# A hybrid attention encoder step: outputs split a head later, reordered steps, and the causal mask added by a product

## The reference, cut to what matters

```
ckv, krope = rmsnorm(lat[:256]), rope(lat[256:])      # lat = rmsnorm(x) @ kv_w_down
k = [ckv @ w_uk | krope] ; v = ckv @ w_uv              # 8 heads, 128 + 64 and 128
q = [q_nope | rope(q_rope)]                            # rmsnorm(q_lat) @ w_uq
s = q @ k.T * scale
s = where(k // 64 <= q // 64, s, -inf)                 # CHUNK = 64
o = softmax(s) @ v * silu(gate)
x = x + rmsnorm(o @ w_out)
```

## Time and profile before

| | |
|---|---|
| median of 3 runs | 616.34 us (614.62 to 617.09) |
| the profiled execution | 617.37 us |
| its span, first to last instruction | 615.6 us |
| busy: PE / PE weight loads | 594.4 (97%) / 571.0 (93%) |
| busy: DVE / ACT / POOL | 368.6 (60%) / 306.3 (50%) / 109.1 (18%) |
| chain that ended last | PE 83%, DVE 9%, ACT 4% |
| mean granted TensorE clock | 0.991 |

### The profile page before, as it was taken

The page is one execution under the profiler, slowest core; times in us unless marked ns, Lnnn a source line. Parts: engine busy times, 40 slices in busy tenths (PEclk is TensorE's granted clock), DMA queues, the critical chain, the costliest instruction groups (busy, mean ns, idle before and its releaser), DMA issues.

```text
span 615.6 us, 11638 instructions
## 1 busy us (share of the span) xinstructions
PE 594.4 (97%) x4446; PEld 571.0 (93%) x4446; DVE 368.6 (60%) x578; ACT 306.3 (50%) x616; POOL 109.1 (18%) x173
## 2 busy tenths in 40 slices
PE   7999999999999999999999999999999959999996
PEld 7999999999999999999999999989988858999996
DVE  5466567554554883257726567468888856754415
ACT  6877473462353472257425515346656627853311
POOL 0100010010020052236706400210000114400002
PEclk8999999999999999999999999999999979999999
DMA  8932362262252163333415322631110144857004
GB/s 290 349 100 69 120 205 70 78 205 69 78 182 92 55 248 123 87 114 126 137 52 154 106 69 69 176 103 30 35 53 18 52 170 138 286 177 274 1 2 172
DMA packets 64888, 75.96 MB, mean 123 GB/s; under 512 B 5568, under 2 KB 55872, under 8 KB 64704
## 3 DMA queue, kind: packets, MB, share of 16 engines
q1 hardware_dynamic: 64832, 75.20, 38.7%
HBM read 62.31 MB, written 10.78 MB: 119 GB/s over the span
## 4 chain that ended last, share of the span: by engine, by line
PE 83%; DVE 9%; ACT 4%; issue 2%; DMA 1%; POOL 0%; SPq 0%; DVEq 0%; ACTq 0%; POOLq 0%
PE bank L1661 25%; PE bank L1662 24%; PE bank L1663 24%; PE bank L1940 3%; ACT prob L1277 2%; DVE pT_lo L1335 1%; PE bank L1708 1%; DVE slab_lo L1335 1%; DVE qN_lo L1335 1%; DVE oT_lo L1335 1%; DVE kN_lo L1335 1%; DVE rows L1331 1%; ACT qS L1064 1%; PE bank L1931 1%; DMA stage<-in_v0g_dram 1%
## 5 line engine op out<-in xcount | busy, mean ns | idle before, releaser
L1661 PE MATMUL bank<-slab_hi,hat_hi 128*128 128x256 f32 (+2 forms) x560 | 161.3, 288 | 2.4 <-DVE slab_lo L1335 2.2
L1662 PE MATMUL bank<-slab_lo,hat_hi 128*128 128x256 f32 (+2 forms) x560 | 160.2, 286 | 0.0
L1663 PE MATMUL bank<-slab_hi,hat_lo 128*128 128x256 f32 (+2 forms) x560 | 160.1, 286 | 0.0
L1661 PEld LDWEIGHTS bank<-slab_hi,hat_hi 128*128 128x128 f32 x560 | 105.9, 189 | 3.9 <-DVE slab_lo L1335 2.6
L1663 PEld LDWEIGHTS bank<-slab_hi,hat_lo 128*128 128x128 f32 x560 | 106.3, 190 | 0.7
L1662 PEld LDWEIGHTS bank<-slab_lo,hat_hi 128*128 128x128 f32 x560 | 105.9, 189 | 0.7
L1335 DVE TENSOR_TENSOR slab_lo<-stage,slab_hi 128x1024 fp32r<-128x1024 f32 (+3 forms) x70 | 83.0, 1186 | 24.9 <-ACT slab_hi L1064 23.4
L1661 PE MATMUL bank<-hat_hi,slab_hi 128*128 128x320 f32 x256 | 79.2, 309 | 0.4 <-DVE krL L1335 0.4
L1662 PE MATMUL bank<-hat_lo,slab_hi 128*128 128x320 f32 x256 | 78.8, 308 | 0.0
L1663 PE MATMUL bank<-hat_hi,slab_lo 128*128 128x320 f32 x256 | 78.7, 308 | 0.0
L1064 ACT ACTIVATE slab_hi<-stage 128x1024 fp32r<-128x1024 f32 (+3 forms) x70 | 71.0, 1014 | 7.2 <-PE bank L1663 2.1
(11 more groups left out here) (326 smaller groups left out, 1326.1 us busy)
## 6 DMA issues: line engine op xcount, KB each, us to landing
stage<-in_a_w_in_dram SPq DMA_DIRECT2D x22, 512.0 KB, 5.0
st_s<-in_state_gla_dram SPq DMA_DIRECT2D x4, 1024.0 KB, 7.0
out_dram<-st_s SPq DMA_DIRECT2D x4, 1024.0 KB, 5.1
stage<-in_a_w_out_dram SPq DMA_DIRECT2D x8, 512.0 KB, 4.3
stage<-in_b_w_in_dram SPq DMA_DIRECT2D x8, 512.0 KB, 4.4
stage<-in_ckvT_dram SPq DMA_DIRECT2D x8, 512.0 KB, 4.1
stage<-in_cache_ckv_dram SPq DMA_DIRECT2D x8, 512.0 KB, 6.1
stage<-in_b_w_out_dram SPq DMA_DIRECT2D x8, 512.0 KB, 4.0
```

The source lines that it names most:

```text
L1661: pe.matmul(out, a[0], b[0], start=first, stop=False)
L1662: pe.matmul(out, a[0], b[1], start=False, stop=False)
L1663: return pe.matmul(out, a[1], b[0], start=False, stop=last)
```

## The change

1. The masked corner is no longer filled by DVE. After the five products of a query tile PE adds a sixth, of two constants of 128 x 128 in which only row 0 is not zero: ones for the first 64 queries, -2^120 for the last 64 keys. They lengthen the table `const_r` by 256 columns.
2. `Oh` h stands a head later, and `O` h behind the slab's low half.
3. `ct`, `cl` of streams 0 and 1 stand a head later. The last `qabs` stands ahead of the last `S`.
4. `st` 0 stands ahead of the last `O`; its scratch `spT` no longer shares memory with `pT`.
5. `glT` stands ahead of `g0` 2. `qT` 0 and `qT` 1 stand among the `cT`. `qn` 0 and `kh` 0 stand ahead of `vh` 1, 1 instead of behind it.

```
-CONST_R, NCONST_R = columns((("cum_p", P + 2), ("cum_s", P + 2)))
+CONST_R, NCONST_R = columns((("cum_p", P + 2), ("cum_s", P + 2), ("early", P), ("late", P)))
...
-    out += [("vg", 1), ("vg", 2), ("g0", 0), ("g0", 1), ("g0", 2), ("glT",), ...
+    out += [("vg", 1), ("vg", 2), ("g0", 0), ("g0", 1), ("glT",), ("g0", 2), ...
...
-    out += [("gb", 3, 0), ("cT", 0), ("cT", 1), ("gb", 3, 1), ("cT", 2), ("cT", 3)]
+    out += [("gb", 3, 0), ("cT", 0), ("cT", 1), ("qT", 0), ("gb", 3, 1), ("cT", 2), ("cT", 3), ("qT", 1)]
     load("uqr")
-    out += [("gb", 2, 0), ("cT", 4)] + [("qT", t) for t in range(NT)] + [("ldt",), ("gb", 2, 1)]
+    out += [("gb", 2, 0), ("cT", 4)] + [("qT", t) for t in range(2, NT)] + [("ldt",), ("gb", 2, 1)]
...
-    out += [("vh", 0, t) for t in range(NP)] + [("vh", 1, 0), ("vh", 1, 1)]
+    out += [("vh", 0, t) for t in range(NP)] + [("vh", 1, 0), ("qn", 0), ("kh", 0), ("vh", 1, 1)]
...
-        elif 4 <= h < 6:
-            out += [("ct", h - 4)]
+        elif 5 <= h < 7:
+            out += [("ct", h - 5)]
+        if h + 1 == HB - 1:
+            out += [("qabs", h + 1)]
...
-        if 0 <= h < HB - 1:
-            out += [("O", h), ("Oh", h)]
+        if 0 < h < HB:
+            out += [("Oh", h - 1)]
         if 0 <= h < 4:
             out += [("plo", ("hd", h + 4), 0)]
-        elif 4 <= h < 6:
-            out += [("cl", h - 4)]
+        elif 5 <= h < 7:
+            out += [("cl", h - 5)]
+        if 0 <= h < HB - 1:
+            out += [("O", h)]
...
+        out += [("st", b)] + [("zr", b + 2)] * (b + 2 < SB)
         if b == 0:
             out += [("O", HB - 1)]
-        out += [("st", b)] + [("zr", b + 2)] * (b + 2 < SB)
...
-                    link(dve.memset(row[0:P // 2, i0 * P:i0 * P + 2 * apart].rearrange("p (j n) -> p j n", n=apart)[:, :, P // 2:P], NEG))
...
-                        last = pe.matmul(o, qS[:, h, q], krL[:, keys], start=False, stop=True)
+                        pe.matmul(o, qS[:, h, q], krL[:, keys], start=False, stop=False)
+
+                        last = pe.matmul(bank[:, j, q], cst_r("early"), cst_r("late"), start=False, stop=True)
```

More of the change, by code:

```diff
@@ L135, in steps @@
     out += [("rq",), ("rr",), ("const",), ("piece", ("qk", 0), 0), ("gf",), ("gfh",), ("gfl",), ("plo", ("qk", 0), 0), ("vg", 0), ("gw",)]
-    out += [("vg", 1), ("vg", 2), ("g0", 0), ("g0", 1), ("g0", 2), ("glT",), ("g0x", 0), ("g0x", 1), ("piece", ("qk", 0), 1)]
+    out += [("vg", 1), ("vg", 2), ("g0", 0), ("g0", 1), ("glT",), ("g0", 2), ("g0x", 0), ("g0x", 1), ("piece", ("qk", 0), 1)]
     out += [("z", u) for u in Z_ORDER] + [("g0x", 2), ("qp", 0), ("plo", ("qk", 0), 1)]
@@ L225, in latent_layer @@
     load(("hd", 1))
-    out += [("vh", 0, t) for t in range(NP)] + [("vh", 1, 0), ("vh", 1, 1)]
+    out += [("vh", 0, t) for t in range(NP)] + [("vh", 1, 0), ("qn", 0), ("kh", 0), ("vh", 1, 1)]
     load(("hd", 2))
-    out += [("qn", 0), ("kh", 0), ("vh", 1, 2)]
+    out += [("vh", 1, 2)]
     prompt_heads(out, load)
@@ L239, in prompt_heads @@
             out += [("piece", ("hd", h + 4), 0)]
-        elif 4 <= h < 6:
-            out += [("ct", h - 4)]
+        elif 5 <= h < 7:
+            out += [("ct", h - 5)]
+        if h + 1 == HB - 1:
+            out += [("qabs", h + 1)]
         if h + 1 < HB:
-            out += [("S", h + 1, 0), ("S", h + 1, 1), ("N", h + 1, 0), ("N", h + 1, 1), ("qabs", h + 1)]
+            out += [("S", h + 1, 0), ("S", h + 1, 1), ("N", h + 1, 0), ("N", h + 1, 1)]
+        if h + 1 < HB - 1:
+            out += [("qabs", h + 1)]
         if h + 2 < HB:
@@ L252, in prompt_heads @@
             out += [("cr", 2), ("ss", 0)]
-        if 0 <= h < HB - 1:
-            out += [("O", h), ("Oh", h)]
+        if 0 < h < HB:
+            out += [("Oh", h - 1)]
         if 0 <= h < 4:
             out += [("plo", ("hd", h + 4), 0)]
-        elif 4 <= h < 6:
-            out += [("cl", h - 4)]
-        elif h == 6:
+        elif 5 <= h < 7:
+            out += [("cl", h - 5)]
+        if 0 <= h < HB - 1:
+            out += [("O", h)]
+        if h == 6:
             out += [("ot", 2)]
@@ L541, in program @@
         const_r = sb("const_r", [P, NCONST_R], fp32r)
-        place[0] += 8 * P
         gain = {n: sb("gain_" + n, [P, k]) for n, k in
@@ L655, in program @@
         prob = [sb(f"prob{i}", [P, NT, P]) for i in range(2)]
-        place[0] = temp_at
-        spT = sb("spT", [P, TOK])
         place[0] = prob_at
         sprob = [sb("sprob1", [P, NT, P])]
+        spT = sb("spT", [P, TOK])
         place[0] = prob_at + 2 * 4 * NT * P
@@ L1614, in _ @@
                     _, h, u = step
-                    i0, i1 = UNITS[u]
-                    apart = 512 + (i1 - i0) * P
-                    link(dve.memset(row[0:P // 2, i0 * P:i0 * P + 2 * apart].rearrange("p (j n) -> p j n", n=apart)[:, :, P // 2:P], NEG))
                     for j, i in enumerate(UNITS[u]):
@@ L1980, in constants @@
     const = [np.eye(P), before, before * same, (i[:, None] // SL % 2 == np.arange(2)[None, :]), np.cos(ang), np.sin(ang)]
-    const_r = [cum_p, cum_s]
+    row = (i == 0).astype(np.float32)[:, None]
+    const_r = [cum_p, cum_s, row * (1 - half.T * 0 - (i >= P // 2)[None, :]), row * np.where(i >= P // 2, NEG, 0.0)[None, :]]
     return [np.ascontiguousarray(np.concatenate(x, axis=1).astype(np.float32)) for x in (const, const_r, turned[:1], turned[1:])]
```

## The result

The changed kernel takes 619.91 us (median of 7 runs, 617.58 to 621.91), the kernel before in the same session 615.47 (7 runs, 614.48 to 617.09). The ratio is 1.0058, 95% interval 1.0034 to 1.0082: slower, by 0.6%. The forecast was 614.8 with a range of 611.6 to 618.8. The profiled execution of the changed kernel has a span of 618.2 us, the one before 615.6.

The account below looks back on a forecast made before the run. PE was taken as the bound, busy 594 of 615.6 us. Heads -1.1, tail -3.5, projections +4.1, prologue -0.5 and `qn` 0, `kh` 0 -0.5 sum to -1.5: 614.8 us from the median 616.34, range 611.6 to 618.8.

Parts of the forecast that it names:

- What bounds the kernel: Whole kernel: PE busy 594 of 615.6 us; almost all its long waits lie where the change works.
- The mask as a product: PE gains 32 products, 0.45 us a head, 3.6 in all (bounds 1.8 and 8.6); DVE loses 16 memsets.
- rival C: Mask products cost PE 0.27 us each instead of 0.11, 5 us more: 619.8; chance 0.06.
- The heads: Heads 0 to 5: PE becomes the bound at 11.33 us, gain 1.6, less 0.45 for `S` 0's masks: -1.1.
- rival D: DVE's list still bounds the heads, which stay at 11.7 us, no gain of 1.6: 616.4; chance 0.10.
- `T` 6 to `sv` 0: Tail: 27.1 us becomes 23.6, old waits replaced by 6.5 us of new ones: -3.5, bounds -5.5 and -1.5.
- rival A: Clock falls at the projections' new wait, +2.4 to +3.4, up to 618.2; tail waits likewise, +2.4 each; chance 0.20.
- The MLA projections: `gb` 3, 1 takes the banks of `gb` 3, 0, so PE idles 3.3 us: +4.1, bounds +5 and 0.
- The prologue: Start: `g0` 2 covers `glT`'s read-out, a wait of 0.90; `glT` itself waits some 0.35: -0.5.
- `qn` 0 and `kh` 0: Ahead of `S` 0: a step earlier, the wait of 0.46 for `kN_lo` goes, covered by a `vh`: -0.5.
- The sum: Whole kernel: -1.1 - 3.5 + 4.1 - 0.5 - 0.5 = -1.5, giving 614.8 from the median; chance 0.50.

Follow-up runs that it names:

- e10: The kernel before with only `Oh` h a head later and `O` h behind the slab's low half; 610.32 us, ratio 0.9913 to the kernel before.
- e7: e3 with the mask by DVE's memset again and the sixth product left out; 607.98 us, ratio 0.9867 to the kernel before.
- e6: The kernel before with the mask product in place of the memset and nothing else; 614.95 us, ratio 0.9986 to the kernel before.
- e3: The changed kernel with `glT` and `qT` 0, 1 both back in their old places; 611.73 us, ratio 0.9919 to the kernel before.
- e2: The changed kernel with `qT` 0 and 1 back behind `cT` 4, all else as changed; 614.01 us, ratio 0.9969 to the kernel before.
- e4: The changed kernel with repeated products of `g0` 1 and transposes of `qT` 0 filling two PE waits; 617.55 us, ratio 1.0024 to the kernel before.
- e1: The changed kernel with `glT` behind `g0` 2 again, all else as changed; 616.08 us, ratio 1.0004 to the kernel before.
- e12: e3 with `gb` 3, 1 on the banks of `gb` 3, 0 and `cT` 2 on those `gb` 3, 1 had, no step moved; 617.16 us.
- e5: The kernel before, unchanged, profiled a second time; 617.14 us in one execution, span 615.4.
- e8: e3 with four steps of the tail moved, mask product kept; 607.74 us, ratio 0.9882 to the kernel before.
- e9: e8 with the mask by DVE's memset and no sixth product, as in e7; 605.19 us, ratio 0.9828 to the kernel before.

## Why the prediction was wrong

**What bounds the kernel**, right: PE, with its waits where the change works.

**The mask as a product**, right in price and wrong in worth. 0.47 for `S` 0 and 11.33 a head against 0.45 and 11.33; rival C had no part. But the working held both numbers that condemn it, 10.57 us a head on DVE and 11.33 on PE, and with the memset kept they would read 10.91 and 10.88. It was never asked which edit earned the heads' gain. e10, e7 and e6 show it: `Oh` alone 4.3 us in the heads, the product a loss of 3.75 beside it and a gain of 0.9 without it.

**The heads**, right: -1.64 for -1.6, and rival D fell. DVE's list had a second gap beside that of 0.83, one of 0.29 for ACT's `prob`, which the working took as full; it changed nothing.

**`T` 6 to `sv` 0**, right in its number partly by luck: 23.55 for 23.6. The waits are 2.0 and 2.88 for the 2.5 and 3.0 taken, and those of 0.6 and 0.4 did not come. But the clock, forecast at its upper level, fell behind the second wait, in every profile with that wait (2.75 to 3.20) but e3's. In e3 `T` 7 to `sv` 0 takes 11.17, in the changed kernel 12.12, so with the clock up the stretch would be 22.6. In e2, e3 and e4 the clock fell behind the first wait too, and `T` 6 to `T` 7 took 13.0 instead of 11.4. So a fall in the tail, which rival A put at 2.4, cost 1.0 or 1.6.

**The MLA projections**, the term of +4.1 right as far as it went: 4.15 without a fall of the clock (e1), waits of 3.13, 0.79, 0.46 for 3.3, 0.9, 0.6. Rival A came true on top of it, at 1.3 to 1.8 and not at every execution, for the 2.4 to 3.4 priced: the work ran at half rate for 2.8 us (337.6 to about 340.4; the 0.78 of the last second is 0.44 low), in e12 for 3.4, not for 4.8 or the whole block. I had kept it out of the likeliest sum because no row decided it, and gave it 0.20. Of the three profiles with that wait unfilled two show the fall (the changed kernel's and e12's) and e1's does not; that it is the commoner case is likely, not shown.

**The prologue**, the step that failed: that `g0` 2 "now covers the read-out of `glT`, a wait of 0.90", and that `glT` itself waits for the low halves of `vg` 0 only "some 0.35", for a term of -0.5. The start of `g0` 2 at 29.9 that it rests on belonged to one execution, in which PE had lost 2.2 us to a late slab and then ran at half rate until about 11 us (granted clock 0.50 from 8 to 10). In e5, the same kernel, PE reaches that point some 2.1 earlier. With PE early, `g0` 2 is what fills the wait for `vv_lo`, and taking it away opens one of 2.7, behind which the clock falls. Measured in the start of `z`: 1.5 for the order and 2.9 for the clock, +4.4 against e1, where -0.5 stood (e2 against e3: +3.1); in the medians 2.3 to 3.8. The late start of the first profile is also why the two profiled spans differ by only 2.6 us and the medians by 4.4.

**`qn` 0 and `kh` 0**, right: the wait of 0.46 is gone, and `cT` 0 to `T` 0 is 0.70 shorter in e7 than before, for the 0.5 forecast.

**The sum.** -1.5 forecast, +4.4 measured, so 5.9 are missing. By the medians, the two edits that e3 undoes cost 8.2 together where 4.1 - 0.5 = 3.6 was forecast: 4.6 of it. All the rest gains 3.9 where 5.1 was forecast: another 1.2 (in e3's profile 0.6 in the tail and 1.0 behind `sv` 0, less what the other stretches gained). The range should have been wider by its own terms: +2.0 for the tail and +3.4 for one fall of the clock give 620.2, not 618.8. The seven times of the changed kernel run from 617.58 at a mean granted clock of 0.994 to 621.91 at 0.985.

## What to carry to other kernels

Before a step is moved away from a place, look at what it covers there, in a second execution as well: a start time that stems from one late slab can make a cover of 2.7 us look like one of 0.35. Where buffers are numbered round-robin, compare the table of who holds what before whom, since two `qT` steps moved up the list cost 4.4 to 5.9 us through a bank. And price the edits of a change singly against the bound that the others leave: the mask product was worth something only while DVE was the bound, and the later `Oh` ended that.

## What the runs showed of the hardware

A wait of a given length does not settle whether the granted clock falls. It stayed up behind 3.12 us in e1 and behind 2.88 in e3, and fell behind 2.88 in e1 and behind 2.00 in e3. Behind 0.88 followed by 0.90, with 0.77 of transposes between, it fell in e8 and stayed at 1.00 in e9. A fall cost 1.0 to 2.9 us each time. That goes with the spread from run to run: 3.8 to 5.9 us over the 12 runs each of e1, e2, e4 and e12, 1.1 over the four of e9, whose waits are all below 1.7. It is not all of it, since e3 and e7 with waits of 2 to 3 us spread over no more than 2.1 (6 and 4 runs), and e4 took 617.38 and 620.47 at the same mean clock of 0.994. In one execution a stretch of unbroken products ran 4% slower at a granted clock of 1.00 and with no wait (e5, 384 products for 400): the granted clock is not all that sets the pace.
